# Turning a table's rows by VectorE in 32 by 32 blocks instead of by TensorE

## What is computed

```
eidx  = ...top 16 experts of each head...
act   = gelu(einsum('thkd,td->thk', expert_u[eidx], xb))
w     = gate * act
out   = einsum('thk,thkd->td', w, expert_v[eidx])
```

## Time and profile before

| | |
|---|---|
| median of 3 runs | 4007.78 us (4001.41 to 4015.57) |
| profiled execution | 3997.62 us, its span 3995.8 us |
| TensorE / VectorE / ScalarE / GpSimd busy in the span | 85% / 75% / 39% / 27% |
| `h2d` loaded (L2595); first dots (L2667) | 2690.4 us; 2954.6 us |
| table pass (L2676) | first value matmul starts at 2975.9 us, last at 3984.7 us |
| L2656, TensorE's turns | 1024, 137.7 us |
| L2718, ScalarE's copies of them | 256, 136.2 us of records |

### The profile page before, as it was taken

One profiled execution on the slowest core, in us unless ns is written; L12 is line 12 of the kernel. 1 busy time (PEld: TensorE's weight loads), 2 busy tenths in 40 slices (PEclk: granted clock), 3 DMA queues, 4 the chain that ended last, 5 costly groups with the idle time before them and its releaser, 6 DMA issues. The chain is left out here.

```text
span 3995.8 us, 48226 instructions
## 1 busy us (share of the span) xinstructions
PE 3411.8 (85%) x15838; PEld 2266.2 (57%) x15838; DVE 2982.0 (75%) x5688; ACT 1577.9 (39%) x3960; POOL 1082.4 (27%) x879
## 2 busy tenths in 40 slices
PE   8989998978877788887677758886879999999998
PEld 6657866534543444455466634344446666666665
DVE  6693114988987788899776789799867777787765
ACT  2313412426753243376533323325852332333232
POOL 0100001342233433322232233332333333333331
PEclk9999998989989899998888878998989999999999
DMA  4614458998889999987798989886999999999996
GB/s 167 114 47 159 136 181 318 396 419 291 323 312 389 388 391 418 373 294 277 296 365 336 385 316 406 329 345 247 379 400 409 416 416 416 414 416 416 411 415 248
DMA packets 307131, 1315.95 MB, mean 329 GB/s; under 512 B 43458, under 2 KB 109474, under 8 KB 200770
## 3 DMA queue, kind: packets, MB, share of 16 engines
q0 software_dynamic: 120272, 854.67, 54.0%
q1 hardware_dynamic: 186226, 458.07, 30.9%
q10 hardware_dynamic: 384, 0.13, 0.0%
HBM read 1252.03 MB, written 58.88 MB: 328 GB/s over the span
## 5 line engine op out<-in xcount | busy, mean ns | idle before, releaser
L1033 POOL DMA_INDIRECT arena<-in_uv,arena x800 | 1027.1, 1284 | 2255.4 <-DVE arena L1199 2014.7
L723 PE MATMUL ps<-arena 128*128 128x256 f32 (+2 forms) x3456 | 1105.7, 479 | 147.5 <-DMA arena<-in_w_stat 78.0
L1189 DVE CUSTOM_DVE_ANT_0 arena<-arena 128x1024 f32<-128x1024 f32 x800 | 973.6, 1219 | 51.7 <-DMA arena<-in_uv,arena 46.8
L1199 DVE SCALAR_TENSOR_TENSOR arena<-arena 128x1024 f32<-128x1024 f32 x736 | 943.1, 1281 | 80.3 <-ACT arena L1290 80.2
L723 PEld LDWEIGHTS ps<-arena 128*128 128x128 f32 x3456 | 675.7, 199 | 533.3 <-issue 321.5
L1281 ACT ACTIVATE arena<-arena 128x2 f32<-128x2 f32 x400 | 81.1, 203 | 1143.8 <-DVE arena L1189 1131.3
L2667 PE MATMUL ps<-arena 128*128 128x256 f32 x2048 | 472.8, 385 | 0.0
L2676 PE MATMUL ps<-arena 128*128 128x512 f32 x1024 | 460.0, 592 | 0.0
L2667 PEld LDWEIGHTS ps<-arena 128*128 128x128 f32 x2048 | 386.4, 194 | 49.5 <-issue 0.5
L2676 PEld LDWEIGHTS ps<-arena 128*128 128x128 f32 x1024 | 194.6, 190 | 191.2 <-issue 184.6
L2797 DVE TENSOR_TENSOR arena<-arena 128x256 f32<-128x256 f32 x128 | 79.8, 623 | 260.9 <-ACT arena L2759 249.8
(11 more groups left out here) (293 smaller groups left out, 3992.9 us busy)
## 6 DMA issues: line engine op xcount, KB each, us to landing
arena<-in_uv SPq DMA_DIRECT2D x256, 512.0 KB, 23.2
arena<-in_w_stat SPq DMA_DIRECT2D x216, 512.0 KB, 7.7
arena<-in_cache_k SPq DMA_DIRECT2D x64, 512.0 KB, 9.9
arena<-in_cache_v SPq DMA_DIRECT2D x64, 512.0 KB, 10.6
arena<-in_w_mov SPq DMA_DIRECT2D x14, 2048.0 KB, 15.0
scr_w<-arena SPq DMA_DIRECT2D x8, 1792.0 KB, 19.6
arena<-scr_w SPq DMA_DIRECT2D x14, 1024.0 KB, 25.6
arena<-in_uv,arena POOLq DMA_INDIRECT x800, 11.4
```

Of the source, the lines that this page charges most:

```text
L723: last = nc.tensor.matmul(ps[:, bank, 0:w], wbuf[m % NWB][:, kc * P:(kc + 1) * P], moving[:, kc, :], start=(kc == 0), stop=(kc == KC - 1))
L1033: pool.indirect_dma_start(ring[s % RING], None, dr["uv"], bass.IndirectOffsetOnAxis(ap=idx[:, g % 4, j:j + 1], axis=0)).then_inc(row_in[s ...
L1189: nc.vector.tensor_tensor_reduce(ring[s % RING][:, 0:D], ring[s % RING][:, 0:D], h2r[:, b % 2, :], 1.0, 0.0, ALU.mult, ALU.add, act_in[:, ...
L1199: nc.vector.scalar_tensor_tensor(accr[:, b % 2, :], ring[s % RING][:, D:2 * D], wgt[:, s % RING:s % RING + 1], accr[:, b % 2, :], ALU.mult ...
```

## The change

VectorE has a transpose of 32 by 32 blocks, which cannot move data between groups of 32 partitions. So the u rows are loaded in another layout: group `a` of 32 partitions gets the quarter `a` of the columns of all 128 rows (four rows, 32 apart, side by side in one partition). One VectorE instruction then turns all 128 blocks of a tile, and partition `32a + i` holds column `256a + 32k + i` in piece `k`. The hidden states `h2d` are loaded in the same order of columns. TensorE's turns, ScalarE's copies and the semaphore `turn_free` go away; `u_in` now waits for VectorE's turn. The turns run two tiles ahead of the dots, behind `weights(e)`.

```diff
                 for j in range(2):
-                    sp.dma_start(h2d[:, :, j * P:(j + 1) * P], scr_t[j]).then_inc(hd_in, 16)
+                    for c in range(KC):
+                        sp.dma_start(h2d[32 * (c // 2):32 * (c // 2) + 32, 4 * (c % 2):4 * (c % 2) + 4, j * P:(j + 1) * P],
+                                     scr_t[j, :, c, :].rearrange("(q i) n -> i q n", i=32)).then_inc(hd_in, 16)
...
                         if e >= NUR:
                             sp.wait_ge(turn_d, e - NUR + 1)
-                        sp.dma_start(u_rows[:, e % NUR, :], dr["uv"][e * P:(e + 1) * P, 0:D]).then_inc(ur_in[e % NUR], 16)
+                        for a in range(4):
+                            sp.dma_start(u_rows[32 * a:32 * a + 32, e % NUR, :].rearrange("j (b x) -> j b x", b=4),
+                                         dr["uv"][e * P:(e + 1) * P, 256 * a:256 * (a + 1)].rearrange("(b j) x -> j b x", b=4)
+                                         ).then_inc(ur_in[e % NUR], 16)
...
-                def turn_rows(e):
-                    pe.wait_ge(ur_in[e % NUR], 16 * (e // NUR + 1))
...
-                    for i in range(KC):
-                        last = nc.tensor.transpose(ps[:, 6 + i // 4, (i % 4) * P:(i % 4 + 1) * P], u_rows[:, e % NUR, i * P:(i + 1) * P],
-                                                   ident[:, :])
-                    last.then_inc(turn_d, 1)
-
                 def expert_dots(e):
-                    pe.wait_ge(turn_free, 2 * e + 2)
+                    pe.wait_ge(turn_d, e + 1)
...
-                def turned_in(e):
...
-                    for i in range(2):
-                        nc.scalar.activation(u_turned[:, e % 2, 4 * i:4 * i + 4, :].rearrange("p c n -> p (c n)"), ps[:, 6 + i, :],
-                                             ACT.Copy).then_inc(turn_free, 1)
...
+                def turn_blocks(e):
+                    dve.wait_ge(ur_in[e % NUR], 64 * (e // NUR + 1))
+                    if e >= 2:
+                        dve.wait_ge(dots2, e - 1)
+                    nc.vector.transpose(u_turned[:, e % 2].rearrange("p (k b) j -> p k b j", k=KC),
+                                        u_rows[:, e % NUR, :].rearrange("p (b k i) -> p k b i", b=4, k=KC)).then_inc(turn_d, 1)
...
+                dve.wait_ge(grid_free, NQ)
+                for e in range(2):
+                    turn_blocks(e)
                 for e in range(NE_T):
                     weights(e)
+                    if e + 2 < NE_T:
+                        turn_blocks(e + 2)
                     peer_dve(dve, beside_tile(e))
```

More of the change, by code:

```diff
@@ L2555, in hybrid_step @@
         AT_CH = 8704 + (NUR + NV) * D
-        chunk, u_turned = lay(AT_CH, [2, 2 * P, SJ]), lay(AT_CH + 4096, [2, KC, P])
+        chunk, u_turned = lay(AT_CH, [2, 2 * P, SJ]), lay(AT_CH + 4096, [2, 4 * KC, 32])
         STORED = 8
@@ L2568, in hybrid_step @@
         names = ("hd_in", "x2_in", "below_d", "ex2_d", "sum2_d", "gate2_d", "t3_ready", "t3_free", "iota_d", "hot_d", "gated_d", "grid_d",
-                 "grid_free", "turn_d", "turn_free", "dots2", "gelu2_d", "wgt2_d", "v_sum", "y2_acc", "y2_sq", "y2_ms", "y2_rt",
+                 "grid_free", "turn_d", "dots2", "gelu2_d", "wgt2_d", "v_sum", "y2_acc", "y2_sq", "y2_ms", "y2_rt",
                  "y2_rc", "y2_done", "y2_out")
-        (hd_in, x2_in, below_d, ex2_d, sum2_d, gate2_d, t3_ready, t3_free, iota_d, hot_d, gated_d, grid_d, grid_free, turn_d, turn_free,
+        (hd_in, x2_in, below_d, ex2_d, sum2_d, gate2_d, t3_ready, t3_free, iota_d, hot_d, gated_d, grid_d, grid_free, turn_d,
          dots2, gelu2_d, wgt2_d, v_sum, y2_acc, y2_sq, y2_ms, y2_rt, y2_rc, y2_done, y2_out) = (rested.pop() for _ in names)
@@ L2666, in expert_dots @@
                     for kc in range(KC):
-                        last = nc.tensor.matmul(ps[:, 4 + e % 2, 0:2 * P], u_turned[:, e % 2, kc, :], h2d[:, kc, :],
+                        last = nc.tensor.matmul(ps[:, 4 + e % 2, 0:2 * P], u_turned[:, e % 2, 4 * kc:4 * kc + 4, :].rearrange("p b j -> p (b j)"), h2d[:, kc, :],
                                                 start=(kc == 0), stop=(kc == KC - 1))
@@ L2692, in _ @@
                     peer_pe(pe, beside_group(q))
-                pe.wait_ge(hd_in, 32)
-                turn_rows(0)
+                pe.wait_ge(hd_in, 32 * KC)
                 for e in range(NE_T + LAG):
-                    if e + 1 < NE_T:
-                        turn_rows(e + 1)
                     if e < NE_T:
@@ L2711, in choice_in @@
                     nc.scalar.activation(turned3[:, j].rearrange("p k n -> p (k n)"), ps[:, j, 0:3 * P], ACT.Copy).then_inc(t3_free, 1)
-                def turned_in(e):
-                    act.wait_ge(turn_d, e + 1)
-                    if e >= 2:
-                        act.wait_ge(dots2, e - 1)
-                    for i in range(2):
-                        nc.scalar.activation(u_turned[:, e % 2, 4 * i:4 * i + 4, :].rearrange("p c n -> p (c n)"), ps[:, 6 + i, :],
-                                             ACT.Copy).then_inc(turn_free, 1)
                 def gates_in(q):
@@ L2751, in _ @@
                     peer_act(act, beside_group(q))
-                turned_in(0)
                 for e in range(NE_T):
-                    if e + 1 < NE_T:
-                        turned_in(e + 1)
                     act.wait_ge(dots2, e + 1)
```

## The result

The changed kernel takes 4307.0 us (median of 6 runs, 4299.4 to 4315.2), the kernel before 4007.3 us (6 runs). The ratio is 1.0752, 95% interval 1.0729 to 1.0775. Forecast were 4172 us and a range of 4030 to 4260: the direction and the place were right, the size was not, and the time lies outside the range.

The account below looks back on a forecast made before the run. The DMA engines were taken to bound the pass at 7.96 us a tile. Narrow u loads, 128 x 1.4 = +179 us, and -6 at the end gave +173 on 3997.6, 4171, taken as 4172; range 4030 to 4260.

Parts of the forecast that it names:

- What bounds the pass: Table pass, last quarter of the kernel: DMA engines set the pace, 7.96 us a tile at 416 GB/s; TensorE waits.
- The term of -6: End of the pass, DMA share 0.72: about 7 tiles are TensorE's, each saving 0.87 us, -6 us.
- VectorE's terms: VectorE in the pass: 1.23 us a transpose, hidden under DMA; its wait for u loads costs no DMA time: 0.
- SyncE: SyncE's queue: four u issues a tile instead of one, 0.33 us each, 1 us more, hidden by waits: 0.
- Packets: u loads on the DMA engines: 1 KB packets instead of 4 KB, +0.17 us a tile.
- Few partitions: u loads on the DMA engines: 32 partitions a load cost 2.1 times, 1.44 us a tile, 1.4 in the sum.
- both readings: Price of loads into 32 partitions: 2.4 times from a trace row, 2.2 times by interpolating between 16 and 128 partitions.
- the four loads: Sample tokens' hidden states, four 128 KB loads into 32 partitions each: 283 GB/s against 418, 2.4 times their price.
- The interpolation: Loads into 16 partitions 3.2 times, 128 partitions 1.0, equal factors each halving: 32 partitions 3.2^(2/3) = 2.2 times.
- the steeper rival: u loads in the pass: DMA loss of 2.0 us a tile, +250 us, 4248 us; chance 0.08.
- TensorE's clock: Rival in the pass: idle TensorE drops to 1.2 GHz, needs 9.7 us a tile, +38, 4210; within the forecast's 0.55.
- The signs: Pass: DMA share 1.0, 340 to 370 GB/s, over 9 us a tile, TensorE idle a quarter, awaiting VectorE; transposes near 1.2 us.

Follow-up runs that it names:

- Experiment 5: Kernel before, with the u table laid out turned by the host, so no engine turns anything and the dots read the loaded tile: 4000.9 us, ratio 0.9985.
- experiment 1: Changed kernel, but each u tile is one wide load from a copy laid out by the host; VectorE still turns: 4003.5 us, ratio 0.9986.
- experiment 6: Kernel before, with each u tile loaded by four loads of 4 KB rows into 32 neighbouring partitions each; TensorE still turns: 4338.0 us, ratio 1.0824.
- experiment 9: Kernel before, with each u tile loaded by four loads, each into every fourth partition, 32 in all: 4008.3 us, ratio 1.0001.
- experiment 11: Changed kernel, with eight u loads a tile instead of four, alternating between lower and upper 64 partitions every 64 KB: 4242.8 us, ratio 1.0578.
- experiment 2: Changed kernel, but each u tile is one load into all 128 partitions in 1 KB packets (other data, only time counts): 4030.1 us, ratio 1.0053.
- Experiment 3: Changed kernel, but the four u loads each put 32 whole 4 KB rows into 32 partitions (only time counts): 4324.6 us, ratio 1.0788.
- Experiment 15: Kernel before, with the pairs beside the tiles moved behind the pass and u in four loads into 32 neighbouring partitions each: 4662.8 us, ratio 1.1650.
- (13): Kernel before, with only the v tiles loaded by four loads into 32 neighbouring partitions each, u wide: 4332.8 us, ratio 1.0825.
- (10): Kernel before, with both u and v tiles loaded by four loads into 32 neighbouring partitions each: 4409.8 us, ratio 1.0994.
- experiment 7: Changed kernel, but each u tile comes by two loads of 64 whole rows into 64 neighbouring partitions each (only time counts): 4339.0 us, ratio 1.0827.
- experiments 14: Kernel before, with all pairs that went beside the tiles moved behind the pass, all loads wide: 4657.2 us, ratio 1.1636.
- experiment 12: Changed kernel, but each of the four u loads carries one 1 KB piece for all 128 partitions: 4708.8 us, ratio 1.1740.

## Why the prediction was wrong

**What bounds the pass: right.** The DMA engines' time sets the pace. Experiment 5 takes TensorE's 0.87 us and ScalarE's copies away, and 9 us are gained that can't be told from zero; experiment 1 has -4 us. The term of -6 agrees with both, and neither proves it.

**VectorE's terms: right.** A transpose takes 1.24 us, 1.23 were taken. The new wait is long (354 us) and costs nothing by itself: experiment 6, which has TensorE wait instead, pays as much.

**SyncE: right in the sum, by another way.** The issues are not 0.33 us each. The source views of the changed kernel's u and v loads (ns min/median/max):

```profile
L2604 SPq DMA_DIRECT2D arena<-in_uv x512: 311/820/11572, 2960.0 to 4263.3; - x171
```

```profile
L2612 SPq DMA_DIRECT2D arena<-in_uv x128: 328/801/12659, 2977.9 to 4277.5; - x128
```

An issue takes 0.8 us in the middle and up to 12.7. With the same number of u loads spread over the partitions (experiment 9) the longest issue is 2.0 us and no time is lost, and experiment 11 has twice the u loads and is faster. So the number of issues is not the bound; that the long ones come from DMA engines that are behind is likely, and not shown.

**Packets: right in size, and left out of the sum.** +0.17 us a tile was worked out; experiment 2 has 22/128 = 0.17, or 0.24 by its pace. The sum's 1.4 us are 1.31 x 1.1 alone. With 0.17 more it would have given about 4193 us, still far too little.

**Few partitions: the step that failed.** It read: "I take a little under both readings, 2.1 times, because the narrow loads are a sixth of the bytes here and were over a third there, so wide packets can fill more holes." For the whole term of 1.4 us the runs have 2.6 us by the pace, or (300 + 6)/128 = 2.4 us in the sum's own way of counting. Without the packets' part that is 2.2 to 2.4 us over 1.31, 2.7 to 2.8 times, more than both readings. Experiment 3, with packets of 4 KB, has 10.9 - 7.96 = 2.9 us, 3.2 times. And the reason given is turned round by the runs: wide packets do not fill holes, they are slowed. The queues' sums show it for the gathers. The packets in the traces, sorted by size, show it for each kind (mean ns of one, between 3000 and 3900 us, to 4200 in the changed kernel):

| | before | 2: u wide, 1 KB | changed | 3: u narrow, 4 KB |
|---|---|---|---|---|
| u tile | 163 | 48 (1 KB) | 71 (1 KB) | 221, u and v together |
| v tile, wide, 4 KB | 163 | 169 | 238 | 221, u and v together |
| gathers, 8 KB | 316 | 320 | 379 | 422 |

*The narrow tile itself: 1.5 times.* 512 packets of 71 ns are 512 x 0.071/16 = 2.3 us of all engines in the changed kernel, against 1.5 us at 48 ns. Experiment 15 has the same 1.5. This part is 0.7 to 0.85 us a tile, beside about 0.2 us for the packets' size.

*The rest is paid by wide packets.* The v tile's 128 packets take 128 x 0.075/16 = 0.6 us more, and the gathers, some 260 packets a tile, 260 x 0.063/16 = 1.0 us more. Neither was edited. Packets' size, narrow tile, v tile and gathers add up to the 2.6 us. Without gathers the whole extra shrinks to 0.85 us (15), against 2.75 us for the same narrow loads with gathers (6). Which tile is narrow makes no difference (13), and a second narrow one adds only 72 us (10), so the price belongs to the mixture. Gathers need not be there at the moment: in a stretch of the changed kernel VectorE waits for u, and hardly a gather is under way. Window, then its queues:

```profile
3618.00:3624.00 6.00, 0.26 (x1) 0.29 (x2) 2.79 (x4) 0.00 (x0) 0.00 (x0) 0.61 1.09 213
```

```profile
q1 hardware_dynamic: 935, 1.28, 108.7%
q0 software_dynamic: 3, 0.00, 0.0%
```

213 GB/s is half of 416, at a DMA share of 1.09: the engines have work, and half of the rate is lost. Of the 1.28 MB, 0.57 are wide packets of 4 KB (by the trace's packets), and these take 303 ns each instead of 163.

Experiments 7 and 9 show what makes a load narrow: 64 neighbours are as bad as 32, and 32 partitions spread by fours cost nothing. It is a matter of which partitions one load reaches. By the formula in the Trainium skill's section cited at experiment 7, 32 or 64 neighbours from 0 on lie behind 8 of 16 ports and a step of 4 reaches all; that there are ports is the account of the Trainium skill, that neighbours cost and spread ones do not is shown here.

Alternating between the halves takes part of the loss back: 4307, 4267, 4243 us with pieces of 256, 128 and 64 KB for one half. One account of the slowed wide packets is that they stand behind narrow ones while the other half has nothing to do. It is a guess: no row shows the order inside an engine, and that link stays open.

The forecast could have seen this in its own rows. In the window of the four loads, the trace's wide packets of 8 KB take 445 ns instead of 316: the loss of 945 KB was already shared with wide traffic, and the narrow loads were a third of the bytes there, not over a third. The interpolation also failed as a method: 3.2^(2/3) put a curve through 16 and 128 partitions, the 16 had packets of 512 bytes (3093 of them in the window of the earlier trace rows), so that their factor is not one of partitions alone, and experiment 7 says that between 64 and 128 there is a step. The row of the four loads said 2.4, nearest of all, and was cut down by an argument; taken as it stood it gave the 4248 us of the steeper rival, and even that is 59 us short. The upper bound of the range came from the same reading and so was too low.

**TensorE's clock: as the rival had it, with no price of its own.** Granted is 0.87 of full speed in the pass instead of 0.99. The value matmuls take 692 ns on average; before it was:

```profile
L2676 PE MATMUL ps<-arena 128*128 128x512 f32 x1024 | 460.0, 592 | 0.0
```

At 7.8 us of work in a tile of 10.55, the slower clock fills idle time.

**The signs.** DMA share near 1, transposes near 1.2 us and a TensorE that is idle a quarter of the time (26%) came true. The rate is 315 GB/s and not 340 to 370, which says again that the loss was dearer. And TensorE waits for v tiles (326 us), hardly for VectorE's turn (32 us).

## What to carry to other kernels

Before a layout splits a load by groups of neighbouring partitions, look whether the DMA engines are full. If they are not, it is free (experiments 14 and 15); if they are, it costs here half as much again for its own bytes, and a slowdown of everybody else's packets that is larger than that. If it has to be split, take every fourth partition, at no cost (experiment 9). Where the layout forbids that, as here, alternating between the lower and the upper half in small pieces (11) takes back 64 of 300 us.

A DMA share near 1 says that the engines have work, not that they move bytes: read it beside GB/s. And where a trace has a row of just the shape that an edit adds, take its price as it stands, and look in the same window what happened to the packets beside it.

When the DMA engines bind a pass, removing another engine's work gains little. Here 111 us of TensorE's queue were worth 9 us at most in the medians, and nothing that can be told from zero.

## What had not been expected of the hardware

- 64 neighbouring partitions a load are no faster than 32 (4339 and 4325 us), and 32 partitions in steps of four are as fast as 128 (ratio 1.0001).
- Narrow loads slow the packets of the other queue: from 281 ns to 336 in the changed kernel and 374 in experiment 3, by a fifth and by a third.
- Four loads a tile over all 128 partitions, with 4 as the slowest dimension of their source, left the DMA engines at a share of 0.72 and cost 701 us (experiment 12).
- An issue on SyncE's queue took up to 12.7 us beside narrow loads; before the change it took 0.33 us in the middle and 1.1 at most, with spread loads (experiment 9) 2.0 at most.
